# One place per query tile for the scores of both attention branches, and a first product that starts on high parts

## The reference, cut to what matters

```python
# 8 query heads, 2 key heads (kv); the selected branch and the window branch
sc = jnp.einsum('bqhgd,bhqkd->bhgqk', qb, kg) * scale
p = masked_softmax(sc, m_sel)
o_sel = jnp.einsum('bhgqk,bhqkd->bqhgd', p, vg)
sc = jnp.einsum('bqhgd,bkhd->bhgqk', qb, kw) * scale
p = masked_softmax(sc, m_win)
o_win = jnp.einsum('bhgqk,bkhd->bqhgd', p, vw)
out = g[0] * o_cmp + g[1] * o_sel + g[2] * o_win
```

## Time and profile before

| | before |
|---|---|
| median of 3 runs | 1680.43 us (1680.42 to 1680.99) |
| the profiled execution: its time | 1681.69 us |
| its span | 1679.9 us |
| PE busy | 1663.3 us, 99% |
| PE weight loads busy | 1441.8 us, 86% |
| DVE busy | 1172.9 us, 70% |
| ACT busy | 758.2 us, 45% |
| POOL busy | 118.2 us, 7% |
| chain that ended last | PE 89%, DVE 5%, DVE sequencer 2%, ACT 2%, DMA 1%, issue 1% |
| TensorE clock granted | 0.999 of full speed |

### The profile page before, as it was taken

How to read it: one execution, slowest core, us unless ns; L and a number is a source line. 1 busy time by engine, 2 the same in 40 slices (tenths; PEclk the granted TensorE clock), 3 DMA queues, 4 the chain that set the end, 5 groups by cost and what they waited for, 6 DMA issues and landing times.

```text
span 1679.9 us, 28691 instructions
## 1 busy us (share of the span) xinstructions
PE 1663.3 (99%) x11302; PEld 1441.8 (86%) x11302; DVE 1172.9 (70%) x1709; ACT 758.2 (45%) x1281; POOL 118.2 (7%) x241
## 2 busy tenths in 40 slices
PE   8999999999999999999999999999999999999998
PEld 7888888788889999988888888887888899999886
DVE  5888888554469898863459888875453788988524
ACT  4334667422345544541344347663222554545423
POOL 5700010000000000000055001000000000000000
PEclk9999999999999999999999999999999999999999
DMA  8563121233632333233274532112244333333232
GB/s 265 160 151 83 58 63 51 55 96 101 190 125 90 112 101 107 83 101 100 89 255 121 132 89 54 56 51 76 88 133 131 112 101 101 101 101 101 88 101 88
DMA packets 68222, 179.00 MB, mean 107 GB/s; under 512 B 14608, under 2 KB 25904, under 8 KB 67840
## 3 DMA queue, kind: packets, MB, share of 16 engines
q1 hardware_dynamic: 42560, 151.01, 29.2%
q10 hardware_dynamic: 23040, 17.83, 4.2%
q0 software_dynamic: 2496, 8.40, 1.8%
HBM read 164.37 MB, written 7.08 MB: 102 GB/s over the span
## 4 chain that ended last, share of the span: by engine, by line
PE 89%; DVE 5%; DVEq 2%; ACT 2%; DMA 1%; issue 1%; ACTq 0%; SPq 0%
PE ps L654 12%; PE ps L656 11%; PE ps L655 11%; PE ps L1149 8%; PE ps L1151 8%; PE ps L1150 8%; PE ps L699 6%; PE ps L701 6%; PE ps L700 6%; PE ps L1033 2%; PE ps L1020 2%; PE ps L1004 2%; DMA raw<-wstream 1%; ACT whi L1198 1%; PE ps L711 1%
## 5 line engine op out<-in xcount | busy, mean ns | idle before, releaser
L1740 DVE TENSOR_TENSOR wlo<-raw,whi 128x1024 fp32r<-128x1024 f32 x170 | 210.8, 1240 | 264.5 <-ACT whi L1198 262.0
L1198 ACT ACTIVATE whi<-raw 128x1024 fp32r<-128x1024 f32 x164 | 173.8, 1060 | 304.5 <-PE ps L701 190.0
L654 PE MATMUL ps<-xh,whi 128*128 128x512 f32 x672 | 266.7, 397 | 1.9 <-DVE wlo L1740 1.2
L656 PE MATMUL ps<-xh,wlo 128*128 128x512 f32 x672 | 262.5, 391 | 1.0 <-issue 1.0
L655 PE MATMUL ps<-xl,whi 128*128 128x512 f32 x672 | 262.3, 390 | 0.3 <-issue 0.3
L654 PEld LDWEIGHTS ps<-xh,whi 128*128 128x128 f32 x672 | 126.2, 188 | 29.6 <-issue 3.5
L656 PEld LDWEIGHTS ps<-xh,wlo 128*128 128x128 f32 x672 | 126.2, 188 | 27.5 <-issue 0.6
L655 PEld LDWEIGHTS ps<-xl,whi 128*128 128x128 f32 x672 | 126.3, 188 | 24.8 <-issue 0.5
L699 PE MATMUL ps<-whi,hh 128*128 128x512 f32 x336 | 131.1, 390 | 0.0
L700 PE MATMUL ps<-wlo,hh 128*128 128x512 f32 x336 | 130.8, 389 | 0.0
L701 PE MATMUL ps<-whi,hl 128*128 128x512 f32 x336 | 130.8, 389 | 0.0
(11 more groups left out here) (442 smaller groups left out, 4027.1 us busy)
## 6 DMA issues: line engine op xcount, KB each, us to landing
raw<-wstream SPq DMA_DIRECT2D x184, 512.0 KB, 3.6
a<-wstream SPq DMA_DIRECT2D x40, 512.0 KB, 4.3
a_x<-wstream SPq DMA_DIRECT2D x40, 512.0 KB, 3.6
w<-w1s SPq DMA_DIRECT2D x16, 512.0 KB, 6.9
sm<-smalls POOLq DMA_DIRECT2D x2, 1060.0 KB, 8.1
xt<-xin ACTq DMA_DIRECT2D x4, 512.0 KB, 6.7
scratch_u<-pa ACTq DMA_DIRECT2D x8, 256.0 KB
toep<-scratch_k ACTq DMA_DIRECT2D x4, 512.0 KB
```

The source lines that it names most:

```text
L654: pe.matmul(ps[:, bank, :], wh, hi[:, k, :], start=first and i == 0, stop=False)
L656: m = pe.matmul(ps[:, bank, :], wl, hi[:, k, :], start=False, stop=last and i == len(blocks) - 1)
L1198: act.activation(whi[:, c % 2, :], raw[:, c % 2, :], ACT.Copy).then_inc(hi_ready, 1)
L1740: dve.tensor_tensor(wlo[:, c % 2, :], raw[:, c % 2, :], whi[:, c % 2, :].bitcast(f32), SUB).then_inc(lo_ready, 1)
```

## The change

- `sbank` and `score_cols`: scores 2 and 3 lie side by side in banks 0 and 1 (2 was in banks 4 and 5), and 3 starts at column n.
- `scores` is called in the even units only, and makes the scores of both branches of a tile. For t < 2 one pair of masks and four products cover both branches (t = 1: 512 columns instead of twice 256). For t = 2 and 3 four masks come first, then four products of each branch. Ahead of them is a wait on s_exp: scores 4 and 5 wait until exps 3 is done, 6 and 7 until exps 5.
- `exps(2)` waits for the maxima of scores 2 and 3, and `max_part(3)` moves from unit 1 to unit 0 on DVE.
- `first_slabs`: zeros four times, the last with 256 columns; then the products of slab 0 with the first 256 tokens in an order of their own, high by high first, each group behind the semaphore of what it reads. Slab 1 is sent for at x_hi 1.
- `first_powers` of layer 0 moves behind `a1_out(0)` and `a1_split(1)`.

```diff
--- before.py
+++ after.py
@@ -406,12 +406,12 @@
         def sbank(i):
-            return 4 if i % 2 == 0 or i % 8 == 1 else 0
+            return 4 if i % 8 in (0, 1, 4, 6) else 0
         def score_cols(i):
             n = P * (i % 8 // 2 + 1)
-            return slice(P, 2 * P) if i % 8 == 1 else slice(0, n)
+            return slice(n, 2 * n) if i % 8 in (1, 3) else slice(0, n)
         def turned_at(i, kv):
@@ -464,7 +464,7 @@
         @block.sync
         def _(sp):
             sp.dma_start(raw[:, 0, :], wstream[0, :, :]).then_inc(raw_loaded[0], 16)
-            sp.wait_ge(x_hi, 2)
+            sp.wait_ge(x_hi, 1)
             sp.dma_start(raw[:, 1, :], wstream[1, :, :]).then_inc(raw_loaded[1], 16)
             def load_slab(n, s, skipped):
@@ -760,14 +760,36 @@
             def first_slabs():
                 pe.wait_ge(toep_zero, 2)
-                for _ in range(5):
-                    pe.matmul(ps[:, 7, :], toep[:, 0, :], toep[:, 0:4, :].rearrange("p g n -> p (g n)"), start=True, stop=True)
-                for c in range(2):
-                    pe.wait_ge(lo_ready, c + 3)
-                    for half in range(2):
-                        for g in range(4):
-                            m = x_quarter(c, half, g, 0)
-                    m.then_inc(slab_done, 1)
+                zeros = toep[:, 0:4, :].rearrange("p g n -> p (g n)")
+                for n in (512, 512, 512, 256):
+                    pe.matmul(ps[:, 7, 0:n], toep[:, 0, :], zeros[:, 0:n], start=True, stop=True)
+                def first_products(part, weights, x):
+                    for k in range(4 * part, 4 * part + 4):
+                        pe.matmul(ps[:, 4, 0:256], weights[:, 0, k * P:k * P + P], x[:, k, 0:256], start=part == 0 and weights is whi and x is xh and k == 0,
+                                  stop=part == 1 and x is xl and k == KD - 1)
+                pe.wait_ge(x_hi, 1)
+                pe.wait_ge(hi_ready, 1)
+                first_products(0, whi, xh)
+                pe.wait_ge(x_ready, 2)
+                first_products(0, whi, xl)
+                pe.wait_ge(x_hi, 2)
+                first_products(1, whi, xh)
+                pe.wait_ge(lo_ready, 3)
+                first_products(0, wlo, xh)
+                first_products(1, wlo, xh)
+                pe.wait_ge(x_ready, 4)
+                first_products(1, whi, xl)
+                for g in range(4):
+                    m = x_quarter(0, 1, g, 0)
+                m.then_inc(slab_done, 1)
+                pe.wait_ge(lo_ready, 4)
+                for half in range(2):
+                    for g in range(4):
+                        m = x_quarter(1, half, g, 0)
+                m.then_inc(slab_done, 1)
             def first_pair(n, at, rt):
@@ -982,28 +1004,29 @@
                 def scores(i):
-                    t, br = i % 8 // 2, i % 2
-                    if t == 0:
+                    t = i % 8 // 2
+                    n = P * (t + 1)
+                    if t < 2:
+                        both = [ps[:, sbank(i) + kv, 0:2 * n].rearrange("p (b n) -> p b n", b=2) for kv in range(2)]
                         for kv in range(2):
-                            pe.matmul(ps[:, 4 + kv, 0:2 * P].rearrange("p (b n) -> p b n", b=2), identb[:, :], bc(dmaskb[:, :], 1, 2), start=True, stop=True)
+                            pe.matmul(both[kv][:, :, P * t:n], identb[:, :], bc(dmaskb[:, :], 1, 2), start=True, stop=True)
                         for kv in range(2):
                             q = q_parts[i // 8][kv]
                             for k in (k_high[kv], k_low[kv]):
-                                m = pe.matmul(ps[:, 4 + kv, 0:2 * P].rearrange("p (b n) -> p b n", b=2), q[:, 0:P], k[:, :, 0:P],
-                                              start=False, stop=k is k_low[kv], skip_group_check=True)
+                                m = pe.matmul(both[kv], q[:, P * t:P * t + P], k[:, :, 0:n], start=False, stop=k is k_low[kv], skip_group_check=True)
                         m.then_inc(s_psum, 2)
                         return
-                    if i % 8 == 2:
-                        pe.wait_ge(s_exp, l * 32 + i)
-                    n = P * (t + 1)
-                    for kv in range(2):
-                        pe.matmul(ps[:, sbank(i) + kv, P * t:n], identb[:, :], dmaskb[:, :], start=True, stop=True)
-                    for kv in range(2):
-                        q = q_parts[i // 8][kv]
-                        for k in (k_high[kv], k_low[kv]):
-                            m = pe.matmul(ps[:, sbank(i) + kv, 0:n], q[:, P * t:P * t + P], k[:, br, 0:n],
-                                          start=False, stop=k is k_low[kv], skip_group_check=True)
-                    m.then_inc(s_psum, 1)
+                    pe.wait_ge(s_exp, l * 32 + i)
+                    for x in (i, i + 1):
+                        for kv in range(2):
+                            pe.matmul(ps[:, sbank(x) + kv, P * t:n], identb[:, :], dmaskb[:, :], start=True, stop=True)
+                    for x in (i, i + 1):
+                        for kv in range(2):
+                            q = q_parts[i // 8][kv]
+                            for k in (k_high[kv], k_low[kv]):
+                                m = pe.matmul(ps[:, sbank(x) + kv, 0:n], q[:, P * t:P * t + P], k[:, x % 2, 0:n],
+                                              start=False, stop=k is k_low[kv], skip_group_check=True)
+                        m.then_inc(s_psum, 1)
                 def turned(i):
@@ -1075,7 +1098,7 @@
                         at, k0, k1 = unit_part(j, u)
                         part_slab(first_slab(j) + at, k0, k1)
                         pe.wait_ge(q_ready, l * 4 + (j + 3))
-                    if i < 30 and u != 7:
+                    if i < 30 and u % 2 == 0:
                         scores(i + 2)
                     if u == 2:
                         pe.wait_ge(cs_ready, l * 4 + (j + 1))
@@ -1330,11 +1353,10 @@
                 act.wait_ge(small_head_in, l * 16 + 16)
                 act.activation(st[:, 0, :], smv("ldt"), ACT.Exp).then_inc(dt_ready, 1)
-                if l == 0:
-                    first_powers()
                 a1_out(0)
                 if l == 0:
                     a1_split(1)
+                    first_powers()
                 a1_out(1)
                 if l == 0:
                     a1_split(2)
@@ -1522,7 +1544,7 @@
                 def exps(i):
                     n = P * (i % 8 // 2 + 1)
-                    act.wait_ge(s_max, l * 32 + (i + 1 + (i % 8 == 0)))
+                    act.wait_ge(s_max, l * 32 + (i + 1 + (i % 8 in (0, 2))))
                     for kv in range(2):
                         x = act.activation(prob[:, i % 2, kv, 0:n], ps[:, sbank(i) + kv, score_cols(i)], ACT.Exp,
                                            bias=tiny[:, 28 + 8 * (i % 3) + kv:29 + 8 * (i % 3) + kv],
@@ -2296,9 +2318,9 @@
                     if u == 6 and j < 3:
                         split_lo(hl_, first_slab(j) + 3)
                         gelu_low(j)
-                    if i < 30 and u != 7:
+                    if i < 30 and u not in (7, 1):
                         max_part(i + 2)
-                    if i < 30 and u == 6:
+                    if i < 30 and u in (6, 0):
                         max_part(i + 3)
                     if u == 0 and j:
                         compressed_in(j, 3)
```

## The result

The kernel after takes 1688.42 us (median of 6 runs, 1686.92 to 1689.43), the kernel before, measured with it, 1680.71 (6 runs, 1680.36 to 1683.74). The recorded ratio is 1.0032, 95% interval 1.0022 to 1.0043: slower, with all of the interval above 0.2%. Applied to 1680.43 us it gives 1685.8 us (1684.1 to 1687.7), where 1684.9 was forecast. The two medians alone lie 7.7 us apart (1.0046), a little outside that interval, so the sign is certain and the size is known to 2 or 3 us only; what follows explains the difference of the two traces. The span of the profiled execution went from 1679.9 to 1685.1 us, +5.2 where the sum said +4.4. The mean granted clock is 0.999 in the one and 0.998 in the other.

A forecast was written before the change was run, and what follows sets the result against it. PE was taken to bound the kernel. Waits of +6.45 us, less 0.2 for joint products and 1.8 at the start, gave +4.4 us: from 1680.43 to 1684.9 us, +0.26%, 8-in-10 range 1679.5 to 1687.5.

The forecast's parts named there:

- What bounds: Whole kernel: PE bounds, busy 99%; DVE and ACT run at most 1 us behind in middle head pairs, so PE pays delays.
- The start up to slab 2: First slabs on PE: first product at about 8.1 us, slab 2 begun at 20.7 instead of 22.63, 1.9 us earlier.
- I keep 1.8 of the 1.9 us.: After the first slabs: nearly all the gain at slab 2 reaches the kernel's end, counted as -1.8 us.
- second chain: DVE's input matrices, 61 to 83 us, then DMA issues and a slab's landing: moves along with PE, slack under 1 us in places.
- The joint products, -0.2: Scores for t = 1: one 1.10 us call replaces two of 0.65 us; net 0.02 to 0.1 us, 8 times, taken as 0.2.
- The rival of wide products at the price of narrow ones: Scores on PE: 512-column products cost 0.12 us like 256-column ones; 1674.6 us, or 1681 with the waits; chance 0.04.
- Unit 0: Scores 2 in j = 1 and 2: DVE's maxima wait for the joint call, so all that follows is 0.5 us late.
- Unit 4: PE stalls 1.0 us for exps 5, delaying gate_out, exps 6 and DVE; 1.55 us per pair, 1.3 in layer 1's j = 2.
- j = 0 and j = 3: Outer head pairs: j = 0 loses 0 to 0.6 us, taken as 0.25, twice; j = 3 loses nothing.
- Only unit 0's delay is paid: Exps 5 end in time for unit 4; j = 1 and 2 cost 0.5 us each, 1680.4 us, no change; chance 0.2.
- no wait grows: Scores: no PE wait grows and unit 0's loss is made up further on; 1678.4 us, not slower; chance 0.12.
- The start gives nothing: First slabs: slab 1 takes too much from x, or idle stretches lower the clock; 1686.7 us; chance 0.12.

The follow-up runs named there:

- the run with the wait alone: Kernel before with the new start, plus a wait for exponentials 5 ahead of scores 6 in unit 4: 1683.38 us, ratio 1.0008.
- common products alone: Kernel after, but joint products for t < 2 only; for t = 2 and 3 each unit puts its own scores, without the wait: 1682.20 us, ratio 0.9998.
- the run with the start alone: Kernel before with only the changes to first_slabs, the earlier slab 1 and the later first_powers: 1682.41 us, ratio 1.0000.

## Why the prediction came out as it did

- **What bounds.** Right in the main: PE is busy 99% of the span in both, and the 0.5 us that unit 0 puts into DVE's chain came out at PE in full (2.12 us in four pairs). The run with the wait alone fits the slack of 0.5 us ahead of DVE's reciprocal.
- **The start up to slab 2.** Right: 8.07 and 20.51 us were forecast as 8.1 and 20.7, the gain as 1.9 and measured as 2.1.
- **"I keep 1.8 of the 1.9 us."** This is the term that was mis-sized: 0.9 was kept. The prediction said that the second chain "hangs on PE's progress at 59 us and so moves along", and knew that GpSimd slows it. DVE did move along at first (2.3 us at the first `ta` of `coef`). But GpSimd's powers don't move, and the overlap with them takes most of the lead: in the ten traces with the new start and all of GpSimd's work the products with `toep` came 0.3 to 1.5 us earlier, 1.0 in the mean.
- **The joint products, -0.2.** Small as forecast, but undersized: 0.12 to 0.35 us a call in the four head pairs where it shows, 0.8 in all. The prediction's own bound of 0.1 us, taken 8 times, is 0.8 and not the "at most 0.5" that it writes. The rival of wide products at the price of narrow ones fell: two masks and four products take 1.14 us at 512 columns in unit 0 of the kernel after (204.52 to 205.66), against the 0.65 us for 256 columns and 1.10 for 512 of the earlier trace rows.
- **Unit 0.** The 0.5 us late maxima were forecast, and 0.5 us in each of four pairs measured (2.12 with common products alone).
- **Unit 4.** The mechanism was right in j = 1 and only in its first half in j = 2; the price was 6.41 instead of 5.95 us in the four together, unit 0 included. By the runs it is made of 2.1 for unit 0, 0.8 for the second score ahead of the slab's part (2.95 - 2.12), and 3.5 for the wait ahead of both (6.41 - 2.95). Part of it lies where the prediction didn't look. The stall of 1.0 us stands in the profile as idle times of 0.69 us at the masks and 0.30 at the weighted sums of unit 3; from start to start, which takes in the latency that idle time leaves out, it is 0.9 and 0.5, so 1.4 us (transposes of unit 4 to masks 1.57 us against 0.71, weighted sums to transposes 1.55 against 1.03). In j = 2 no wait at the transposes of unit 7 shows, where over 0.5 us was forecast. There it isn't DVE's chain behind `gate_out` that decides: in layer 0 PE has lost its 1.6 us already at the masks (from the weighted sums of unit 3 to the masks of unit 4 3.34 us, before 1.73), and the run that only moves `gate_out` back (1.68 us in j = 2, against 1.57 and 1.55) won nothing there. The longest wait for the exponentials is this one:

```profile
259.88 0.40 PE L1022 MATMUL ps<-dmaskb,identb 128*128 128x128 bf16 x4 [1.06 <-ACT prob L1549]
```

- **j = 0 and j = 3.** Forecast +0.5 and 0; measured -0.43 and +0.27 in j = 0, -0.05 and +0.25 in j = 3. Together nothing.
- **What no step had:** the kernel before paused for 0.98 us at 940.58 in its trace, the kernel after didn't. That alone is more than the 0.7 us that come back between the layers, and such pauses come in kernels with and without the change (see the last section), so I don't count it to the change. Without it the two traces would be 6.2 us apart.
- **The sum.** -0.9 + 6.41 - 0.2 (j = 0) + 0.2 (j = 3) - 0.7 (between the layers) + 0.3 (other stretches) = 5.1 of 5.2 us. The forecast's +4.4 took 0.9 too much for the start and had 0.5 too little for the waits; the 0.7 of j = 0 and the 0.7 between the layers took most of that back. So the sum fits better than its terms, and that is luck: 0.7 us of it is a pause in the trace of the kernel before.
- **The rivals.** "Only unit 0's delay is paid" and "no wait grows" fell with the masks' waits. "The start gives nothing" was half true by another mechanism than the one named.

## What to carry to other kernels

Putting two pieces of work at one place on the bounding engine saved 0.1 to 0.35 us a time here, and it moves everything that was queued between them; here that was a slab's end, on which another engine's queue hung. So look at what stands behind the later of the two, and put the wait between the pieces and not ahead of both: that place was worth 3.5 of 6.4 us. Two works on DVE and GpSimd that overlap by accident are a hidden term: a gain upstream moves the one into the other. And a cost is best read from the start of the same instruction in two traces: the idle times of the profile came to 1.0 us where 1.4 were lost.

## What the runs showed of the hardware

PE pauses now and then without a cause that the profile shows, in the middle of a run of like products: 0.9 to 1.5 us, at 107 to 109 us or at 940.5 us, the same stretch of the program in the two layers. Seven such pauses are in 6 of the 14 traces, of kernels with and without the change, and in the run with the start alone there were both (0.93 at 107.25, 1.34 at 940.52). They take up a gain of 1 us in a single trace. The traces hold a clue to them. Each of the seven ends 2.3 to 2.7 us after a transfer of the kind "instruction" has begun on DMA queue q8, one of 89 in the kernel after. At 107 to 109 us this transfer begins 1.4 to 2.1 us after the first product with `toep` in the five traces that have the pause there, and at the latest 0.9 us after it in the nine that don't. In the second layer the traces don't part so cleanly. So PE may be waiting for instructions that are loaded late; no run tried it, and the cause stays open.
